# Experts in plain fp32 on column groups, each matrix loaded by halves of its rows, results added by five indirect transfers

## The chip, the cores and the metric

The kernel runs on one core of a Trainium2 chip. The metric is device time in microseconds for one execution of the whole program. Before the change the median of three runs is 3200.23 us (3194.36 to 3200.39). Numbers of views and waits come from one profiled execution.

## What is computed

One inference step of a two-layer backbone for 512 sample tokens and 128 prompt tokens of width 1024. Each layer has a mixer (four branches, gates, an output product) and then a feed-forward part of 16 experts, which is what the change is about:

```
aff = softmax(tok @ router_w)                       # per token over 16 experts
top_aff, top_idx = top_k(aff.T, cap)                # each expert takes 64 sample and 16 prompt tokens
xe  = tok[top_idx]
hid = silu(xe @ w_gate[e]) * (xe @ w_up[e])         # 1024 -> 1024
ye  = (hid @ w_down[e]) * top_aff
out = zeros.at[top_idx].add(ye)                     # a token can be taken by several experts
```

Everything is fp32. An expert has three matrices of 1024 x 1024, 4 MB each; the 16 experts of a layer are 201 MB of weights, read once per layer.

## The kernel before

The program is a loop over two layers, each a row of stages with a barrier between them: norm, projections, latent heads, attention, ssm, merge, norm, `router` (line 1709), `choose` (1838), `experts` (1878), `add_experts` (2142). Every engine has its own instruction list, and semaphores order them.

`router` writes the token rows to `tok_rows` in DRAM, clears `sum_rows` in DRAM and starts the first expert loads. `choose` finds for every expert the 80 token numbers (`rows`, 64 of samples and then 16 of prompts) and their weights. `experts` does the products. `add_experts` reads `sum_rows` back and adds it to x.

In `experts` the 80 tokens of an expert are the stationary operand and the weights stream past as the moving one, 512 columns at a time. A plain fp32 matmul is avoided: a weight is split into a high part in fp32r (ScalarE's copy, line 2045) and the rest (VectorE's subtraction, line 2095), the tokens and the hidden rows likewise (2049 and 2100, 2061 and 2119), and three fp32r matmuls (1999 to 2001) replace one.

The unit of work is half the columns of one matrix: 2 MB, loaded by one transfer of SP (`load_expert`, line 247, pieces of 2 KB) into one of four slots of `expert_raw`. `unit` (1993) does it in two halves of k, 24 matmuls in all. Six units are an expert. The order on TensorE for expert e is: up(e), gate(e+1) with the transposes of e's hidden rows between its two units, down(e), and the transposes of the tokens of e+2. SP loads into a slot once VectorE has finished the low parts of the unit in it (`lo_ready`).

Between the products: ScalarE takes tanh of the gate sums (2053), VectorE multiplies by the gate (2106) and by the up sums (2113), TensorE transposes the hidden rows (2008), ScalarE scales the result by the token's weight into `ye` (2072). POOL gathers token rows by an indirect transfer (1967), two experts ahead, and adds `ye` to `sum_rows` by another one that accumulates in DRAM (1978), 80 rows of 4 KB; before the next gather it waits for that add to land.

Names in the traces: `h` is the memory in which the gathered tokens, `ye` and the hidden rows lie; `ps` is PSUM; `w_hi`, `w_lo`, `xe_hi`, `hid_hi` and so on are the split parts. `Modulation.products` (338) and the attention's `values` (967) already use groups of 32 and of 64 columns of TensorE.

## Time and profile before

| | |
|---|---|
| median of 3 runs | 3200.23 us |
| profiled execution | 3198.26 us |
| its span, first to last instruction | 3196.4 us |
| TensorE busy | 2791.0 us (87%), 17628 matmul records |
| VectorE busy | 2016.8 us (63%) |
| ScalarE busy | 1449.4 us (45%) |
| POOL busy | 416.3 us (13%) |
| DMA | 644.97 MB, mean 202 GB/s |
| mean granted TensorE clock | 0.93 of 2.4 GHz |

The span is nearly the whole time, so a stage's length can be read from the trace directly. Busy TensorE is not TensorE at its peak, since matmuls overlap one another; the spacing of starts is what tells how fast it goes. A fp32 matmul appears as two records, a fp32r matmul and a transpose as one. The tables give instructions their line in the kernel; windows are in us from the span's start.

### The profile page before, as it was taken

The page shows a single profiled execution, that of the slowest core. Times are in us where ns is not written, and L with a number is a line of the kernel's source. Part 1 is how long each engine was busy: PE and PEld are TensorE (multiplying, and loading weights), DVE is VectorE, ACT ScalarE, POOL GpSimd, SP SyncE. Part 2 cuts the span into 40 slices and gives each one's busy share as a digit, 9 for nine tenths or more (in the row PEclk, how much of TensorE's full clock was granted, in tenths as well). Part 3 has the DMA queues.
Part 4 walks back from the last instruction along what each step waited for, and adds up shares of the span by engine and source line. Part 5 has one row for each costly group of instructions (what it writes and reads, how often), then busy time and mean ns, then how long its engine had stood idle before and what let it go on. Part 6 is the DMA issues. An engine that isn't in the chain of part 4 may idle for free. (4 is left out here: it accounts for less than half of the span.)

```text
span 3196.4 us, 44902 instructions
## 1 busy us (share of the span) xinstructions
PE 2791.0 (87%) x17628; PEld 2189.9 (69%) x17628; DVE 2016.8 (63%) x2629; ACT 1449.4 (45%) x1672; POOL 416.3 (13%) x150
## 2 busy tenths in 40 slices
PE   4997999797886999999669889996978589999994
PEld 3995878696764666666459767886878466666662
DVE  2225656756626998998542265566665478988983
ACT  3112544432223777777331134443321257777771
POOL 1001000010010233433010100000100103334310
PEclk7998999898987999999889989998989789999997
DMA  6211212135736999999432112222283779999992
GB/s 234 80 41 63 65 54 65 45 87 199 302 136 260 367 389 387 390 386 386 158 115 74 54 47 56 61 59 62 75 336 145 279 255 384 386 393 384 384 354 74
DMA packets 378679, 644.97 MB, mean 202 GB/s; under 512 B 13072, under 2 KB 124816, under 8 KB 377616
## 3 DMA queue, kind: packets, MB, share of 16 engines
q1 hardware_dynamic: 372368, 621.71, 53.6%
q0 software_dynamic: 6144, 20.98, 2.8%
q8 instruction: 112, 1.84, 0.2%
q14 instruction: 55, 0.45, 0.0%
HBM read 591.13 MB, written 51.51 MB: 201 GB/s over the span
## 5 line engine op out<-in xcount | busy, mean ns | idle before, releaser
L2095 DVE TENSOR_TENSOR w_lo<-expert_raw,w_hi 128x2048 fp32r<-128x2048 f32 x384 | 868.0, 2287 | 90.5 <-ACT w_hi L2045 90.2
L2045 ACT ACTIVATE w_hi<-expert_raw 128x2048 fp32r<-128x2048 f32 x384 | 736.7, 1920 | 337.3 <-PE ps L2001 278.4
L1999 PE MATMUL ps<-w_hi,xe_hi 128*80 128x512 f32 x1024 | 408.2, 399 | 11.2 <-DVE xe_lo L2100 11.2
L2000 PE MATMUL ps<-w_lo,xe_hi 128*80 128x512 f32 x1024 | 404.8, 395 | 0.0
L2001 PE MATMUL ps<-w_hi,xe_lo 128*80 128x512 f32 x1024 | 400.6, 391 | 0.0
L1967 POOL DMA_INDIRECT h<-tok_rows,rows x32 | 263.8, 8242 | 289.7 <-DMA sum_rows<-h,rows 183.1
L539 PE MATMUL ps<-h_hi,in_w_hi 128*128 128x320 f32 x640 | 199.6, 312 | 41.3 <-DVE h_lo L591 41.3
L1999 PEld LDWEIGHTS ps<-w_hi,xe_hi 128*80 128x80 f32 x1024 | 152.4, 149 | 92.4 <-DVE xe_lo L2100 11.7
L818 PE MATMUL ps<-h_hi,attention_gate_w_hi 128*128 128x320 f32 x640 | 206.7, 323 | 9.1 <-DVE attention_gate_w_lo L805 9.1
L2001 PEld LDWEIGHTS ps<-w_hi,xe_lo 128*80 128x80 f32 x1024 | 152.6, 149 | 86.3 <-issue 1.8
L1584 PE MATMUL ps<-branch_mix_hi,merge_w_hi 128*128 128x320 f32 x512 | 165.9, 324 | 51.9 <-DVE merge_w_lo L1663 45.3
L1999 PE MATMUL ps<-w_hi,hid_hi 128*80 128x512 f32 x512 | 204.1, 399 | 3.3 <-DVE hid_lo L2119 3.3
L2000 PEld LDWEIGHTS ps<-w_lo,xe_hi 128*80 128x80 f32 x1024 | 152.7, 149 | 76.9 <-issue 1.4
L2000 PE MATMUL ps<-w_lo,hid_hi 128*80 128x512 f32 x512 | 203.4, 397 | 0.0
L2001 PE MATMUL ps<-w_hi,hid_lo 128*80 128x512 f32 x512 | 201.3, 393 | 0.0
L540 PE MATMUL ps<-h_lo,in_w_hi 128*128 128x320 f32 x640 | 199.3, 311 | 0.0
L541 PE MATMUL ps<-h_hi,in_w_lo 128*128 128x320 f32 x640 | 198.9, 311 | 0.0
L819 PE MATMUL ps<-h_lo,attention_gate_w_hi 128*128 128x320 f32 x640 | 198.9, 311 | 0.0
L820 PE MATMUL ps<-h_hi,attention_gate_w_lo 128*128 128x320 f32 x640 | 198.8, 311 | 0.0
L585 DVE TENSOR_TENSOR in_w_lo<-in_raw,in_w_hi 128x2048 fp32r<-128x2048 f32 (+1 forms) x24 | 55.1, 2297 | 183.7 <-ACT in_w_hi L603 183.7
L1066 DVE TENSOR_REDUCE row_max<-ps 128x1 f32<-128x640 f32 (+1 forms) x128 | 88.5, 692 | 116.7 <-PE ps L944 116.7
L1585 PE MATMUL ps<-branch_mix_lo,merge_w_hi 128*128 128x320 f32 x512 | 161.9, 316 | 0.0
(305 smaller groups left out, 5447.7 us busy)
## 6 DMA issues: line engine op xcount, KB each, us to landing
expert_raw<-in_exp_w_gate SPq DMA_DIRECT2D x64, 2048.0 KB, 10.8
expert_raw<-in_exp_w_up SPq DMA_DIRECT2D x64, 2048.0 KB, 10.2
expert_raw<-in_exp_w_down SPq DMA_DIRECT2D x64, 2048.0 KB, 11.2
merge_mod_raw<-in_mod_w SPq DMA_DIRECT2D x16, 2048.0 KB, 11.7
in_raw<-in_w_mix SPq DMA_DIRECT2D x20, 1024.0 KB, 5.3
attention_gate_raw<-in_w_in SPq DMA_DIRECT2D x80, 256.0 KB, 3.4
gate_tanh_back<-gate_rows SPq DMA_DIRECT2D x64, 320.0 KB, 8.0
n_mod_raw<-in_mod_w SPq DMA_DIRECT2D x8, 2048.0 KB, 15.4
```

The source lines that it names most:

```text
L539: pe.matmul(dst, whi[:, s, k, cols], h_hi[:, k, a:z], start=(k == 0), stop=False)
L540: pe.matmul(dst, whi[:, s, k, cols], h_lo[:, k, a:z], start=False, stop=False)
L541: last = pe.matmul(dst, wlo[:, s, k, cols], h_hi[:, k, a:z], start=False, stop=(k == KD - 1))
L818: pe.matmul(self.out, self.whi[:, m % 3, k, :], self.h_hi[:, kk, toks], start=(kk == 0), stop=False)
L819: pe.matmul(self.out, self.whi[:, m % 3, k, :], self.h_lo[:, kk, toks], start=False, stop=False)
L820: last = pe.matmul(self.out, self.wlo[:, m % 3, k, :], self.h_hi[:, kk, toks], start=False, stop=(kk == KD - 1))
L1967: pool.indirect_dma_start(out=xe[:, e % 2, :], out_offset=None, in_=io["tok_rows"], in_offset=bass.IndirectOffsetOnAxis(rows[:, e:e + 1], ...
L1999: pe.matmul(ps[0:SLOTS, bank, :], hi[:, k, :], whi[:, s, w, :], start=(k == 0), stop=False)
L2000: pe.matmul(ps[0:SLOTS, bank, :], hi[:, k, :], wlo[:, s, w, :], start=False, stop=False)
L2001: last = pe.matmul(ps[0:SLOTS, bank, :], lo[:, k, :], whi[:, s, w, :], start=False, stop=(k == KD - 1))
L2045: act.activation(whi[:, (2 * i + kh) % SPLIT], raw[:, i % RAW, KH * kh:KH * kh + KH], ACT.Copy).then_inc(hi_ready, 1)
L2095: v.tensor_tensor(wlo[:, s], raw[:, i % RAW, KH * kh:KH * kh + KH], whi[:, s].bitcast(F32), ALU.subtract).then_inc(lo_ready, 1)
```

## The change

The split is gone. Tokens and hidden rows are used in fp32, and so are the weights, straight from `expert_raw`. To make up for the slower fp32 pass, the two kinds of tokens go separately. The 64 sample tokens are stationary in a group of 64 columns of TensorE, and the two halves of a matrix's columns (512 each) go to the two groups: `samples`. The 16 prompt tokens, padded with zeros to 32, use groups of 32 columns, and the four quarters (256 each) go to the four groups: `prompts`. The sums of an expert then lie in PSUM as 128 partitions by 768: 512 with samples (the partition tells token and half) and 256 with prompts (token and quarter). The gate arithmetic works on that shape, the hidden rows are transposed in six blocks of 128 and not in eight of 80, and the result is added from that shape: one indirect transfer for the samples, which sees `sum_rows` as rows of 512, and four for the prompts, which see it as rows of 256.

A load now fetches half the rows of a matrix (four slices of k, all 1024 columns, pieces of 4 KB), into one of six slots of `expert_raw`, which go by pairs: gate of expert 0 and afterwards every down in the first, up in the second, the other gates in the third. Four of them and not two are started at the router's end. SP loads a slot once TensorE has used it (`used`). At the start of the stage SP copies `rows` and `weight` to the partitions where the groups need them (nine small transfers), VectorE clears the padding and works out the numbers of half and quarter rows, and ScalarE waits for the copies before its first work.

```diff
-IN_RAW, EXPERT_RAW = [P, 2, KD, 2 * P + 4], [P, 4, KD, 512]
+IN_RAW, EXPERT_RAW = [P, 2, KD, 2 * P + 4], [P, 6, KD // 2, D]
...
+SLOT_COLS = CAP_S + 32
+EXPERT_LOADS = (NE + 1, NE, NE - 1)
 def load_expert(sp, io, g, layer, e, matrix, half, slot):
     src = io[("exp_w_gate", "exp_w_up", "exp_w_down")[matrix]][bass.ds(layer, 1)]
     src = src[:, e:e + 1] if isinstance(e, int) else src[:, bass.ds(e, 1)]
-    columns = slice(half * 512, (half + 1) * 512)
-    sp.dma_start(g["expert_raw"][:, slot], src.rearrange("l e (k p) n -> p (l e k) n", p=P)[:, :, columns]).then_inc(
+    k = half * (KD // 2)
+    sp.dma_start(g["expert_raw"][:, slot], src.rearrange("l e (k p) n -> p (l e k) n", p=P)[:, k:k + KD // 2, :]).then_inc(
...
-            for u in range(2):
-                load_expert(sp, io, g, layer, 0, u // 2, u % 2, u)
+            first = [(e, matrix, u) for e, matrix in ((0, 0), (0, 1), (1, 0)) for u in range(2)]
+            for slot in range(2):
+                load_expert(sp, io, g, layer, *first[slot], slot)
...
+        xt = sb("xe_t", [P, 2, KD, WIDE])
+        ht = sb("hid_t", [P, HID // P, P])
+        hid = sb("hid", [P, 2, HID])
+        yq = sb("y_quarters", [P, 2, HID])
+        rows_s, rows_p = sb("rows_sample", [P, NE], mybir.dt.uint32), sb("rows_prompt", [CAP_P, 5, NE], mybir.dt.uint32)
+        weight_s, weight_p = (sb(n, [P, NE]) for n in ("weight_sample", "weight_prompt"))
...
         def _(sp):
-            def load(e, matrix, half, slot):
-                load_expert(sp, io, g, layer, e, matrix, half, slot)
+            sp.wait_ge(blank, 1)
+            for half in range(2):
+                lo = 64 * half
+                copies.start(sp, rows_s[lo:lo + CAP_S], rows[0:CAP_S])
+                copies.start(sp, weight_s[lo:lo + CAP_S], weight[0:CAP_S])
+            copies.start(sp, rows_p[:, 4], rows[CAP_S:SLOTS])
+            for r in range(4):
+                copies.start(sp, weight_p[32 * r:32 * r + CAP_P], weight[CAP_S:SLOTS])
+            def load(e, matrix, pair, done):
+                for u in range(2):
+                    sp.wait_ge(used, done + u)
+                    load_expert(sp, io, g, layer, e, matrix, u, 2 * pair + u)
             def expert(e, q, j, before_last, last_one):
-                if last_one:
-                    return
-                for u in range(UNITS):
-                    sp.wait_ge(lo_ready, halves(e, u + 1))
-                    slot = part(j, u) % RAW
-                    if u < NEXT0:
-                        load(e, DOWN, u, slot)
-                    elif u < DOWN0:
-                        load(e + 1, UP, u - NEXT0, slot)
-                    elif before_last:
-                        load(e + 1, DOWN, u - DOWN0, slot)
-                    else:
-                        load(e + 2, GATE, u - DOWN0, slot)
-            for u in range(LEAD):
-                sp.wait_ge(lo_ready, 2 * (u + 1))
-                load(1, GATE, u, u)
+                load(e, DOWN, 0, e * 6 + 1)
+                if not last_one:
+                    load(e + 1, UP, 1, e * 6 + 3)
+                    if not before_last:
+                        load(e + 2, GATE, 2, e * 6 + 5)
...
+            pool.wait_ge(pieces_ready, 6)
             for e in range(NE):
                 if e + 2 < NE:
                     pool.wait_ge(xe_turned, e + 1)
                     gather(e + 2)
-                pool.wait_ge(ye_ready, e + 2)
-                pool.indirect_dma_start(out=io["sum_rows"], out_offset=bass.IndirectOffsetOnAxis(rows[:, e:e + 1], 0),
-                                        in_=ye[:, e % 2, :], in_offset=None, compute_op=ALU.add).then_inc(rows_added, 16)
-                pool.wait_ge(rows_added, layer * (16 * NE) + 16 * (e + 1))
+                pool.wait_ge(y_copied, e + 2)
+                pool.indirect_dma_start(out=io["sum_rows"].rearrange("t (a n) -> (t a) n", a=2),
+                                        out_offset=bass.IndirectOffsetOnAxis(rows_s[:, e:e + 1], 0),
+                                        in_=yq[:, e % 2, 0:512], in_offset=None, compute_op=ALU.add).then_inc(rows_added, 16)
+                for r in range(4):
+                    pool.indirect_dma_start(out=io["sum_rows"].rearrange("t (a n) -> (t a) n", a=4),
+                                            out_offset=bass.IndirectOffsetOnAxis(rows_p[:, r, e:e + 1], 0),
+                                            in_=yq[32 * r:32 * r + CAP_P, e % 2, 512:HID], in_offset=None, compute_op=ALU.add).then_inc(rows_added, 16)
+                pool.wait_ge(rows_added, layer * (80 * NE) + 80 * (e + 1))
...
-            def unit(e, j, u, bank, hi, lo):
-                for kh in range(2):
-                    s = (2 * part(j, u) + kh) % SPLIT
-                    pe.wait_ge(lo_ready, halves(e, u) + (kh + 1))
-                    for k in range(KH * kh, KH * kh + KH):
-                        w = k % KH
-                        pe.matmul(ps[0:SLOTS, bank, :], hi[:, k, :], whi[:, s, w, :], start=(k == 0), stop=False)
-                        pe.matmul(ps[0:SLOTS, bank, :], hi[:, k, :], wlo[:, s, w, :], start=False, stop=False)
-                        last = pe.matmul(ps[0:SLOTS, bank, :], lo[:, k, :], whi[:, s, w, :], start=False, stop=(k == KD - 1))
-                    last.then_inc(split_free, 1)
-            def turn_hidden(e):
+            def samples(pair, u, bank, left):
+                for k in range(u * KH, (u + 1) * KH):
+                    for half in range(2):
+                        pe.matmul(ps[64 * half:64 * half + 64, bank, :], left(k), raw[:, 2 * pair + u, k % KH, 512 * half:512 * half + 512],
+                                  start=(k == 0), stop=(k == KD - 1))
+            def prompts(pair, u, bank, left):
+                for k in range(u * KH, (u + 1) * KH):
+                    for q in range(4):
+                        last = pe.matmul(ps[32 * q:32 * q + 32, bank, 0:256], left(k), raw[:, 2 * pair + u, k % KH, 256 * q:256 * q + 256],
+                                         start=(k == 0), stop=(k == KD - 1))
+                last.then_inc(used, 1)
...
+            def products(pair, bank, left, nth, between=None):
+                for u in range(2):
+                    loaded(pair, u, nth)
+                    samples(pair, u, bank, left[0])
+                    if u == 1 and between:
+                        between()
+                    prompts(pair, u, bank + 1, left[1])
...
+            def turn_hidden(e, j):
                 pe.wait_ge(hid_ready, e + 1)
-                pe.wait_ge(ye_ready, e + 1)
-                for k in range(KD):
-                    last = pe.transpose(ps[:, 6 + k // 4, (k % 4) * SLOTS:(k % 4 + 1) * SLOTS], hid[:, k * P:(k + 1) * P],
-                                        cst[0:SLOTS, C_ID:C_ID + SLOTS])
+                pe.wait_ge(y_copied, e + 1)
+                for b in range(HID // P):
+                    last = pe.transpose(both(D_BANK)[:, b * P:(b + 1) * P], hid[:, j, b * P:(b + 1) * P], cst[:, C_ID:C_ID + P])
                 last.then_inc(hid_turned, 1)
...
-                for i in range(2):
-                    unit(e, j, UP0 + i, 2 + i, xhi[:, j], xlo[:, j])
+                products(1, U_BANK, tokens(j), q * 32 + 16 * (j + 1))
                 if last_one:
-                    turn_hidden(e)
+                    turn_hidden(e, j)
                 else:
-                    pe.wait_ge(xlo_ready, e + 2)
+                    pe.wait_ge(xt_ready, e + 2)
                     pe.wait_ge(gated, e + 1)
-                    unit(e, j, NEXT0, 0, xhi[:, 1 - j], xlo[:, 1 - j])
-                    turn_hidden(e)
-                    unit(e, j, NEXT0 + 1, 1, xhi[:, 1 - j], xlo[:, 1 - j])
-                pe.wait_ge(hlo_ready, e + 1)
-                for i in range(2):
-                    unit(e, j, (NEXT0 if last_one else DOWN0) + i, 6 + i, hhi, hlo)
+                    products(2, G_BANK, tokens(1 - j), q * 32 + 16 * (j + 1), lambda: turn_hidden(e, j))
+                pe.wait_ge(ht_ready, e + 1)
+                products(0, D_BANK, (lambda k: ht[:, k % 4, 64 * (k // 4):64 * (k // 4) + 64],
+                                     lambda k: ht[:, 4 + k % 2, 32 * (k // 2):32 * (k // 2) + 32]), q * 32 + 16 * (j + 2))
...
+                act.activation(ht[:].rearrange("p a b -> p (a b)"), both(D_BANK), ACT.Copy).then_inc(ht_ready, 1)
...
+                nth = bass.ds(e, 1) if not isinstance(e, int) else slice(e, e + 1)
+                act.activation(yq[:, j, 0:512], ps[:, D_BANK, :], ACT.Copy, scale=weight_s[:, nth])
+                act.activation(yq[:, j, 512:HID], ps[:, D_BANK + 1, 0:HID - 512], ACT.Copy, scale=weight_p[:, nth]).then_inc(y_copied, 1)
...
+            act.wait_ge(blank, 2)
+            act.wait_ge(copies.sem, 16 * 9)
...
+            v.memset(weight_p[:], 0.0).then_inc(blank, 1)
+            v.memset(xt[:, :, :, SLOTS:WIDE], 0.0).then_inc(blank, 1)
+            v.wait_ge(copies.sem, 16 * 9)
+            for half in range(2):
+                part = rows_s[64 * half:64 * half + CAP_S]
+                v.tensor_scalar(part, part, 2.0, float(half), ALU.mult, ALU.add).then_inc(pieces_ready, 1)
+            for r in range(4):
+                v.tensor_scalar(rows_p[:, r], rows_p[:, 4], 4.0, float(r), ALU.mult, ALU.add).then_inc(pieces_ready, 1)
```

How the lists of instructions change, at the two places that matter most. TensorE, inside an expert, around the transposes of the hidden rows (`ps` is PSUM, `cst` the identity, `h` the hidden rows). Before:

```order
L1999 MATMUL ps<-w_hi,xe_hi 80x512
L2000 MATMUL ps<-w_lo,xe_hi 80x512
L2001 MATMUL ps<-w_hi,xe_lo 80x512
L2008 MATMUL ps<-cst,h 128x80 x8
L1996 REGISTER_ALU
L1999 MATMUL ps<-w_hi,xe_hi 80x512
L2000 MATMUL ps<-w_lo,xe_hi 80x512
L2001 MATMUL ps<-w_hi,xe_lo 80x512
```

After (`xe_t` and `hid_t` are the transposed tokens and hidden rows, and x8, x16 are runs of equal rows):

```order
L1994 MATMUL ps<-expert_raw,xe_t 64x512 x8
L2000 MATMUL ps<-expert_raw,xe_t 32x256 x16
L1994 MATMUL ps<-expert_raw,xe_t 64x512 x8
L2024 MATMUL ps<-cst,hid 128x128 x6
L2000 MATMUL ps<-expert_raw,xe_t 32x256 x16
L2006 ISA
L1994 MATMUL ps<-expert_raw,hid_t 64x512 x8
L2000 MATMUL ps<-expert_raw,hid_t 32x256 x16
L1994 MATMUL ps<-expert_raw,hid_t 64x512 x8
L2000 MATMUL ps<-expert_raw,hid_t 32x256 x16
```

Runs of three 80 x 512 matmuls are replaced by runs of eight 64 x 512 and sixteen 32 x 256 ones, in turn, and the transposes now stand between samples and prompts of the gate's second half.

POOL, the first experts of the stage (`h` takes the gathered tokens). Before:

```order
L1967 DMA h<-tok_rows,rows 80x1024 x3
L1978 DMA sum_rows<-h,rows 640x1024
L1980 ISA
L1967 DMA h<-tok_rows,rows 80x1024
L1978 DMA sum_rows<-h,rows 640x1024
L1980 REGISTER_ALU
```

After (`y_quarters` is the scaled result in its 128 by 768 shape):

```order
L1958 DMA h<-tok_rows,rows 80x1024 x3
L1970 DMA sum_rows<-y_quarters,rows_sample 1280x512
L1974 DMA sum_rows<-y_quarters,rows_prompt 2560x256 x4
L1977 ISA
L1958 DMA h<-tok_rows,rows 80x1024
L1970 DMA sum_rows<-y_quarters,rows_sample 1280x512
L1974 DMA sum_rows<-y_quarters,rows_prompt 2560x256 x4
L1977 REGISTER_ALU
```

Each expert's one add to `sum_rows` has become one and four more.

## Rows read from the trace of the kernel before

**Rows 1.** Stages: busy us (count) of PE, PEld, DVE, ACT, POOL; clock, DMA share, GB/s

```profile
1100.00:1508.00 408.00, 408.00 (x1911) 267.18 (x1910) 366.51 (x191) 308.94 (x191) 146.68 (x24) 1.00 1.05 388
```

**Rows 2.** Who waited for whom, 1050 to 1500 us (total, times, longest)

```profile
ACT w_hi L2045 <- PE ps L2001: 108.2, 131, 0.8
```

**Rows 3.** Timeline, two experts (start us, us, engine, line, operation)

```profile
1199.78 0.39 PE L2001 MATMUL ps<-w_hi,xe_lo 128*80 128x512 f32 x1
...
1214.94 0.39 PE L2001 MATMUL ps<-w_hi,xe_lo 128*80 128x512 f32 x1
...
1201.46 2.35 POOL L1978 DMA_INDIRECT sum_rows<-h,rows  x1 [14.92 <-ACT h L2072]
...
1235.66 2.35 POOL L1978 DMA_INDIRECT sum_rows<-h,rows  x1 [15.01 <-ACT h L2072]
```

**Rows 4.** Timeline, PE, transposes of the hidden rows

```profile
1215.17 0.72 PE L2008 MATMUL ps<-cst,h 80*128 80x80 f32 x8
1215.68 0.43 PE L1999 MATMUL ps<-w_hi,xe_hi 128*80 128x512 f32 x1
```

**Rows 5.** Timeline, start of the expert stage in layer 0

```profile
1006.36 1.33 PE L1989 MATMUL ps<-cst,h 80*128 80x80 f32 x8 [6.01 <-DMA h<-tok_rows,rows]
...
1008.80 0.68 ACT L2049 ACTIVATE xe_hi<-ps 128x640 fp32r<-128x640 f32 x1
...
1013.28 0.71 PE L1999 MATMUL ps<-w_hi,xe_hi 128*80 128x512 f32 x1 [5.59 <-DVE xe_lo L2100]
```

**Rows 6.** DMA issues: KB each, median us from issue to landing

```profile
router_w<-in_router_w SPq DMA_DIRECT2D x2, 64.0 KB, 2.4
```

**Rows 7.** Timeline, end of the expert stage in layer 0

```profile
1550.94 0.39 PE L2001 MATMUL ps<-w_hi,xe_lo 128*80 128x512 f32 x1
...
1555.52 1.21 DVE L2113 SCALAR_TENSOR_TENSOR h<-h,ps 80x1024 f32<-80x1024 f32 x1
1556.78 1.33 PE L2008 MATMUL ps<-cst,h 80*128 80x80 f32 x8 [5.46 <-DVE h L2113]
...
1559.77 0.72 PE L1999 MATMUL ps<-w_hi,hid_hi 128*80 128x512 f32 x1 [1.65 <-DVE hid_lo L2119]
...
1574.94 1.40 POOL L1978 DMA_INDIRECT sum_rows<-h,rows  x1 [18.04 <-ACT h L2072]
1584.09 4.45 SPq L2154 DMA_DIRECT2D sum_tok<-sum_rows  x5
```

**Rows 8.** Timeline, PE, plain fp32 at full width, latent heads

```profile
295.91 5.34 PE L721 MATMUL ps<-wukv,kt 128*128 128x256 f32 x24
```

**Rows 9.** Timeline, PE, narrow products between wide ones in the merge

```profile
780.10 0.31 PE L1586 MATMUL ps<-branch_mix_hi,merge_w_lo 128*128 128x320 f32 x1
780.34 1.96 PE L338 MATMUL ps<-merge_mod_raw,silu 128*32 128x128 f32 x64
782.22 0.41 PE L1584 MATMUL ps<-branch_mix_hi,merge_w_hi 128*128 128x320 f32 x1
```

**Rows 10.** Timeline, PE, pairs of 64 columns in the attention

```profile
322.66 0.38 PE L954 MATMUL ps<-cst,x 128*128 128x128 f32 x2
322.98 1.31 PE L967 MATMUL ps<-x,v 128*64 128x128 f32 x20
324.22 0.33 PE L954 MATMUL ps<-cst,x 128*128 128x128 f32 x1
```

**Rows 11.** Timeline, PE, row groups of 64 and 32 in the attention

```profile
405.86 0.49 PE L944 MATMUL ps<-kn,qn 64*128 64x128 f32 x4
406.28 0.49 PE L944 MATMUL ps<-kt,qr 32*128 32x128 f32 x4
```

**Rows 12.** Busy time in windows of 5 us (as rows 1)

```profile
965.00:970.00 5.00, 4.10 (x37) 3.44 (x36) 3.09 (x9) 3.23 (x5) 0.00 (x0) 1.00 1.02 419
...
1205.00:1210.00 5.00, 5.00 (x23) 3.22 (x22) 3.35 (x3) 3.32 (x3) 0.00 (x0) 1.00 1.05 342
1210.00:1215.00 5.00, 5.00 (x24) 3.19 (x23) 5.00 (x3) 3.69 (x2) 4.29 (x1) 1.00 1.05 409
```

More of the change, by code:

```diff
@@ L1747, in _ @@
                 sp.dma_start(io["tok_rows"][t * P:(t + 1) * P, :], htok[:, t, :]).then_inc(rows_out, 16)
-            for u in range(2, EXPERT_RAW[1]):
-                load_expert(sp, io, g, layer, 0, u // 2, u % 2, u)
+            for slot in range(2, EXPERT_RAW[1]):
+                load_expert(sp, io, g, layer, *first[slot], slot)
             sp.wait_ge(rows_out, 16 * 2 * NT)
@@ new lines, in loaded, with tokens @@
+            def loaded(pair, u, nth):
+                pe.wait_ge(raw_loaded[2 * pair + u], layer * (16 * EXPERT_LOADS[pair]) + nth)
+            def products(pair, bank, left, nth, between=None):
[5 more added lines that the diff above has]
+                    prompts(pair, u, bank + 1, left[1])
+            def tokens(j):
+                return (lambda k: xt[:, j, k, 0:CAP_S]), (lambda k: xt[:, j, k, CAP_S:WIDE])
@@ L2032, in _ @@
-            for i in range(LEAD):
-                unit(0, 0, i - LEAD, i, xhi[:, 0], xlo[:, 0])
+            pe.wait_ge(xt_ready, 1)
+            products(0, G_BANK, tokens(0), 16)
             turn_tokens(0, 1)
@@ L2038, in _, with tokens @@
         def _(act):
-            def split_hi(e, q, j, u):
-                i = part(j, u)
-                act.wait_ge(raw_loaded[i % RAW], layer * (16 * NE * UNITS // RAW) + (q * (16 * 2 * UNITS // RAW) + 16 * (i // RAW + 1)))
-                for kh in range(2):
-                    act.wait_ge(split_free, halves(e, u) + (kh + 1))
-                    act.activation(whi[:, (2 * i + kh) % SPLIT], raw[:, i % RAW, KH * kh:KH * kh + KH], ACT.Copy).then_inc(hi_ready, 1)
-            def tokens_hi(nth, j):
+            def tokens(nth, j):
@@ L2055, in expert, with gate @@
+            def gate(done, j):
+                act.wait_ge(used, done)
+                act.activation(hid[:, j, :], both(G_BANK), ACT.Tanh, scale=0.5).then_inc(gate_tanh, 1)
             def expert(e, q, j, before_last, last_one):
+                act.wait_ge(hid_turned, e + 1)
+                act.activation(ht[:].rearrange("p a b -> p (a b)"), both(D_BANK), ACT.Copy).then_inc(ht_ready, 1)
                 if not last_one:
[L2057 to L2058 removed]
@@ L2070, in expert @@
-                act.wait_ge(split_free, halves(e, DOWN0 if last_one else UNITS) + SPLIT)
+                    gate(e * 6 + 6, 1 - j)
+                act.wait_ge(used, e * 6 + (6 if last_one else 8))
                 act.wait_ge(ye_free, e + 1)
-                act.activation(ye[:, j, :], pair(6, SLOTS, D), ACT.Copy, scale=weight[:, bass.ds(e, 1)] if not isinstance(e, int)
-                               else weight[:, e:e + 1]).then_inc(ye_ready, 1)
+                nth = bass.ds(e, 1) if not isinstance(e, int) else slice(e, e + 1)
@@ L2103, in gate @@
-            def gate(nth):
+            def gate(nth, j):
                 v.wait_ge(gate_tanh, nth)
-                v.scalar_tensor_tensor(out=hid, in0=hid, scalar=1.0, in1=pair(0, SLOTS, FF), op0=ALU.add, op1=ALU.mult).then_inc(gated, 1)
+                v.scalar_tensor_tensor(out=hid[:, j, :], in0=hid[:, j, :], scalar=1.0, in1=both(G_BANK), op0=ALU.add, op1=ALU.mult).then_inc(gated, 1)
             def expert(e, q, j, before_last, last_one):
-                if not last_one:
-                    split_lo(e, j, NEXT0)
-                v.wait_ge(split_free, halves(e, NEXT0) + SPLIT)
+                v.wait_ge(used, e * 6 + 4)
```

110 lines of the change are left out of this document (22 added, 88 removed).

## Prediction

> **What bounds the kernel now.** I began with the table of stages. The expert stage (lines 1878 to 2139), which is all that the change touches besides its first loads, runs from about 1000 to 1584 us in layer 0, and again at the end of layer 1. In its steady part TensorE is busy for all of 408 us at the full granted clock of 1.00 (2.4 GHz), while the DMA engines show a share of 1.05 and 388 GB/s [rows 1]. Both look full, so the waits decide. ScalarE, which opens every weight, waits 131 times for TensorE to free a split buffer [rows 2], and no engine waits for a weight load in that stretch. TensorE is the engine that sets the pace.
>
> One expert takes 1235.66 - 1201.46 = 34.2 us, and from the first to the last matmul shown there are 66 steps in 15.16 us, 0.2297 us each [rows 3]. An expert has 3 products x 48 matmuls: 144 x 0.2297 = 33.1 us; its two times eight transposes take 0.51 us each time (and 0.05 us on the matmul behind them) [rows 4]: 34.2 in all, nothing missing. From the first matmul to the end of the last "up" product it is 1550.94 + 0.23 - 1013.28 = 537.9 us [rows 5, 7]. I call this stretch the body.
>
> **The body after the change.** Every product loses its 48 fp32r matmuls of 512 columns. In their place are, for each of 8 slices of k, two fp32 matmuls of 512 columns in column groups of 64 (the samples) and four of 256 columns in groups of 32 (the prompts). All of the splitting on ScalarE and VectorE goes too, but that was hidden work and is costed at nothing.
>
> Do such groups run beside one another? An fp32 matmul leaves two records, and at full width 24 of 256 columns take 5.34 us [rows 8]: 0.22 us each, 2 cycles of 2.4 GHz a column and a little. A record of 128 columns is 106.7 ns. Sixty-four such records in groups of 32 take 782.22 - 780.34 = 1.88 us, the way in excluded [rows 9]; one behind the other they would need 6.8 us, four at a time 1.71. Twenty records in groups of 64 take 1.24 us against 2.13 in a row and 1.07 in pairs [rows 10]. So both kinds overlap fully. The 1.88 us in groups of 32, less 0.09 for the way out, are 16 steps of 0.112 us, some 6 ns over 106.7; I carry 6 ns a step.
>
> One product is then 16 steps x (426.7 + 6) ns for the samples and 16 x (213.3 + 6) ns for the prompts: 6.92 + 3.51 = 10.43 us, against 48 x 0.2297 = 11.03 before. The body holds 47 products (16 gate, 16 up, 15 down): 490.2 us. Token transposes stay, 16 x 0.51 = 8.2 us. Those of the hidden rows become six of 128 columns instead of eight of 80: 0.51 x (6 x 128)/(8 x 80) = 0.61 us, 15 times, 9.2 us.
>
> New is the change between widths of column groups: samples, prompts, samples, prompts makes four changes for a product, and each of 31 groups of transposes adds one: 4 x 47 + 31 = 219. **Their price is the term that I know least.** Going in, the matmul at 780.10 should be done at 780.25 and the narrow one starts at 780.34: 0.09 us [rows 9]. The last transpose before the pairs starts at 322.77, is done at 322.88, and the pair starts at 322.98: 0.10 us; going out, 1.24 - 1.07 - 10 x 0.006 = 0.11 us [rows 10]. On the other side stand short stretches between row groups of 64 and 32: two steps of 0.107 us take 406.28 - 405.86 = 0.42, so 0.2 us a change [rows 11]. There the second step also waits for a 128-column weight load; the new steps of 213 and 427 ns are long enough to hide theirs. I take 0.10 and keep 0.20 as the upper end: 219 x 0.10 = 21.9 us.
>
> Of the old body, 47 products (518.2 us) and 31 times 0.56 us of transposes leave 2.3 us, which I put down to its start at 1.2 GHz (the first matmul is 0.71 us long [rows 5], one at 2.4 GHz 0.39 [rows 3]); the new body starts as cold. Body after: 490.2 + 8.2 + 9.2 + 21.9 + 2.3 = 531.8 us, against 537.9: **-6.1 us a layer**.
>
> **Will the weights come in time?** An expert moves 12.58 MB of weights and 0.66 MB of gathered and scattered rows. The new body gives it (531.8 - 2.3)/15.7 = 33.8 us, so 392 GB/s. The rows show 409 GB/s with the present 2 KB pieces when only weights move, 342 in a window with a scatter, and 419 in a window of 4 KB rows [rows 12]. Pieces become 4 KB, and six halves of a matrix are held instead of four. With all six loaded at the start the PE is five loads, some 28 us, ahead; even if an expert's transfers took 1 us more than the products, 15 us of that would be used. I charge nothing. The skill has a rule against this: the Trainium skill (DMA: Bandwidth & Descriptors, Specifications) gives a limit of some 358 GB/s for a core from HBM, at which an expert's 13.24 MB would take 37 us and transfers, not products, would bind both kernels. The trace disagrees, with 388 GB/s held over 408 us [rows 1].
>
> **The start of the stage.** Before, the first product waits for ScalarE, busy with splits, and for the low half of the tokens: transposes from 1006.36 to 1007.69, ScalarE's high half of 0.68 us, and only at 1013.28, released by VectorE's xe_lo, the first product [rows 5]. Now one ScalarE copy of 0.68 us is enough, so 1008.5 at best. But ScalarE also waits for nine small copies of rows and weights that SP issues. Five issues take 4.45 us in the row of the summed tokens [rows 7], 0.89 each, and a small load lands in 2.4 us [rows 6]: from 1001 that is 1011.4, and the first product at 1012.5. The five are 512 KB transfers and these are 1 to 4 KB, so I lean to the low end, 1009.6: **-3.7 us a layer** (bounds -0.8 and -4.8). Queued behind that wait on ScalarE stands only the first tokens' copy; POOL's gathers do not wait for it.
>
> **The tail.** From the end of the last "up" to the last scatter's issue it is 1574.94 - 1551.17 = 23.8 us: VectorE is still splitting and starts the gate product at 1555.52, transposes 1556.78, hi and lo, first matmul 1559.77, again at 1.2 GHz (0.72 us long) [rows 7]. From there 15.2 us are 48 x 0.2297 = 11.0, 2.3 for the clock and 1.8 for the end of the pipeline, the scaled copy and the issue. After: gate product 0.1 + 0.91 (1.21 x 768/1024), transposes 0.8, one copy 0.9 (0.68 x 768/640 and a start), the down product 10.4 + 0.4, and 1.8 again: 15.3 us, if idle times of 1 us keep the clock up. **-8.5 us a layer**; -6.2 if the clock falls.
>
> Then five indirect adds stand in the place of one, issued one behind the other on POOL. One of 80 rows took 1.40 us with VectorE quiet [rows 7] and 2.35 with it busy [rows 3]; four more of 16 rows cost between nothing (their landing overlaps) and 5.6 us. I take **+3**. In the steady part five of even 2.35 us are 12 us of POOL's 34, and the next expert's products cover them.
>
> **Sum.** -6.1 - 3.7 - 8.5 + 3 = -15.3 us a layer, -30.6 for both. The profiled execution took 3198.3 us (2 us under the median of the three runs), so 3167.7. With half of that offset the forecast is **3169 us**. About 0.2% (6 us) is what a measurement of this kernel can tell from no change.
>
> **Rivals.**
> The changes of width cost 0.2 us, not 0.1. For it: that is what the shortest stretches show [rows 11], and nothing in the trace goes from 64 to 32 columns and back every two or three microseconds. Against it: [rows 9, 10]. It adds 0.1 x 219 x 2 = 44 us: 3213, slower. It decides from 0.17 us a change, where the gain is gone (30/438 above 0.10). The Trainium skill (TensorEngine Tiling (Array Packing), Key Properties) says that changing the tiling mode, unlike changing the tile, drains TensorE; it names no price, and by that rule each of the 219 is paid in full. The trace agrees that each one costs something. Chance 0.18.
>
> The transfers become the bound. The scatter goes from 80 pieces of 4 KB to 128 of 2 KB and 64 of 1 KB, and the dip around a scatter is already deep [rows 12]. A window with one lacks (409 - 342) GB/s x 5 us = 0.34 MB, 0.8 us, and its own 0.33 MB take as much: 1.6 us. If that goes by pieces (x 2.4, +2.2 us) and 4 KB weight pieces are no faster, an expert's transfers need some 36.4 us; over 15 experts they fall 39 us behind, the head start covers 28, and 11 us a layer stay: 3169 + 22 = 3191, about no change on either side of 0.2%. Against it: 419 GB/s in the 4 KB window. Chance 0.14.
>
> Groups of 64 with 512 columns do not overlap (the trace has them with 128 only). Samples would cost double, 3 x 6.9 us an expert: +650 us, 3820. Chance 0.02, against [rows 10].
>
> **Numbers.** The forecast's case has 0.66. Its own range is 3152 (steps without the 6 ns, the scatters hidden) to 3192 (0.14 us a change, a cold tail). Taking in the rivals except the last, the range is 3152 to 3213. Faster by over 0.2%: 0.66; within: 0.14; slower: 0.20.
>
> **What would show it.** Right: a period of about 33.8 us between the scatters of two experts, TensorE with idle time only where the width changes, first product near 1009.6 in stage time, some 15 us from the last up to the scatter. A period of 36 with gaps between narrow and wide matmuls is the first rival; TensorE waiting for expert_raw is the second. I am wrong outright if the products alone show more than 10.8 us each.

## The result, and the profile after

The changed kernel took **3188.1 us** (median; 3186.1 to 3190.5), the kernel before 3199.2 us beside it: a ratio of 0.9968, 95% interval 0.9958 to 0.9978. It is faster by 11 us, or 0.3%, where 30 us were forecast. The gain is small, but the interval lies wholly below 1. The profiled execution took 3189.6 us (before: 3198.3), its span is 3187.5.

First the page of the changed kernel, as far as it answers to the table of before:

```profile
PE 2786.0 (87%) x22172; PEld 1893.9 (59%) x22172; DVE 1096.5 (34%) x2197; ACT 723.6 (23%) x1320; POOL 325.2 (10%) x278
...
L1974 POOL DMA_INDIRECT sum_rows<-y_quarters,rows_prompt x128 | 165.7, 1295 | 39.0 <-issue 39.0
```

VectorE and ScalarE have lost the splits. POOL has gained 128 small adds of 1.3 us. Its total fell all the same, from 416 to 325 us, because a gather's record (line 1967 before, 1958 now) is 0.95 us long on average where it was 8.24. No run isolates why, and POOL was not the bound.

The table of stages, for the stretch of [rows 1] (columns as there):

```profile
1100.00:1508.00 408.00, 408.00 (x3616) 158.06 (x3612) 22.90 (x24) 39.19 (x60) 90.44 (x71) 1.00 1.03 387
```

and POOL's timeline, two samples' adds one expert apart (start, duration, instruction; before: [rows 3]):

```profile
1195.76 1.56 POOL L1970 DMA_INDIRECT sum_rows<-y_quarters,rows_sample  x1 [20.28 <-ACT y_quarters L2067]
...
1229.96 1.56 POOL L1970 DMA_INDIRECT sum_rows<-y_quarters,rows_sample  x1 [19.99 <-ACT y_quarters L2067]
```

An expert takes 1229.96 - 1195.76 = 34.20 us, exactly what it took before. TensorE is still busy all the time at 1.00, and the DMA share is as full as it was. So the steady part gained nothing. TensorE's timeline shows an expert from its second "up" half on (a fp32 matmul counts twice here: samples x16 are 8 matmuls and prompts x32 are 16, four slices of k each; x6 are the hidden rows' transposes, x8 the tokens'):

```profile
1200.35 3.65 PE L1994 MATMUL ps<-expert_raw,xe_t 128*64 128x512 f32 x16
1203.94 1.93 PE L2000 MATMUL ps<-expert_raw,xe_t 128*32 128x256 f32 x32
1205.80 3.65 PE L1994 MATMUL ps<-expert_raw,xe_t 128*64 128x512 f32 x16
1209.39 1.93 PE L2000 MATMUL ps<-expert_raw,xe_t 128*32 128x256 f32 x32
1211.25 3.65 PE L1994 MATMUL ps<-expert_raw,xe_t 128*64 128x512 f32 x16
1214.84 0.88 PE L2024 MATMUL ps<-cst,hid 128*128 128x128 f32 x6
1215.64 1.93 PE L2000 MATMUL ps<-expert_raw,xe_t 128*32 128x256 f32 x32
...
1228.40 0.77 PE L1986 MATMUL ps<-cst,h 80*128 80x80 f32 x8
1229.11 3.22 PE L1994 MATMUL ps<-expert_raw,xe_t 128*64 128x512 f32 x14
```

From start to start, four slices of samples take 1203.94 - 1200.35 = 3.59 us and four of prompts 1.86: a product is 10.90 us, against 11.03 before. The hidden rows' transposes take 0.80, the tokens' 0.71: 3 x 10.90 + 1.51 = 34.2.

The start of the stage in layer 0 (before: [rows 5]); TensorE's timeline, then ScalarE's:

```profile
1005.89 1.33 PE L1986 MATMUL ps<-cst,h 80*128 80x80 f32 x8 [6.02 <-DMA h<-tok_rows,rows]
1009.39 6.57 PE L1994 MATMUL ps<-expert_raw,xe_t 128*64 128x512 f32 x16 [2.17 <-ACT xe_t L2052]
1015.89 1.93 PE L2000 MATMUL ps<-expert_raw,xe_t 128*32 128x256 f32 x32
```

```profile
1008.56 0.70 ACT L2052 ACTIVATE xe_t<-ps 128x640 f32<-128x640 f32 x1 [36.87 <-DMA weight_prompt<-weight]
```

The nine small copies do hold ScalarE, by about a microsecond. The first product starts 3.50 us behind the first transposes, against 6.92 before. Its samples take 6.50 us instead of 3.59, at a granted clock of 0.50 (1.2 GHz) up to 1013 us, behind a stretch in which TensorE was mostly idle.

The end of the stage in layer 0: TensorE, POOL, and the queue's first load of the next stage (before: [rows 7]):

```profile
1545.23 1.93 PE L2000 MATMUL ps<-expert_raw,xe_t 128*32 128x256 f32 x32
1548.24 0.87 PE L2024 MATMUL ps<-cst,hid 128*128 128x128 f32 x6 [1.08 <-DVE hid L2088]
1550.09 3.65 PE L1994 MATMUL ps<-expert_raw,hid_t 128*64 128x512 f32 x16 [0.97 <-ACT hid_t L2060]
```

```profile
1562.45 1.55 POOL L1970 DMA_INDIRECT sum_rows<-y_quarters,rows_sample  x1 [16.83 <-ACT y_quarters L2067]
1564.31 1.30 POOL L1974 DMA_INDIRECT sum_rows<-y_quarters,rows_prompt  x1 [0.30 <-issue]
...
1569.11 1.29 POOL L1974 DMA_INDIRECT sum_rows<-y_quarters,rows_prompt  x1 [0.30 <-issue]
```

```profile
1580.63 2.52 SPq L2117 DMA_DIRECT2D sum_tok<-sum_rows  x5
```

From the last "up" (its end, 1547.09) to the first add it is 15.4 us, with the clock kept at 1.00, against 23.8 before. But from that add to the next stage's load it is 18.2 us, against 1584.09 - 1574.94 = 9.15 before. The sum for layer 0, each from its own rows:

| us, layer 0 | forecast | measured |
|---|---|---|
| start (start of TensorE's wait for the gather to first product: 12.9, now 9.5) | -3.7 | -3.4 |
| body (first product to end of last "up": 537.9, now 537.7) | -6.1 | **-0.2** |
| tail (end of last "up" to first add: 23.8, now 15.4) | -8.5 | -8.4 |
| adds (first add to next load: 9.15, now 18.2) | +3 | **+9.0** |
| sum | -15.3 | -3.0 |

In layer 1 the same four are -3.7, -1.7, -8.4 and +9.3 (its adds take 18.2 us, 8.9 before); the body does better there by 1.5 us because the first samples take 4.99 us and not 6.50. Two terms of the four are off: the body by 5.9 and 4.4 us, the adds by 6.0 and 6.3, 22.6 us for both layers. Missing are 19.5 us by the medians and 21.9 by the profiled executions (8.7 gained of 30.6), so nothing of size lies elsewhere.

### The profile page after: what moved, and what is told of

The parts are those of the page before. It is cut to its first block and busy times, and to the rows that moved or that the text cites. A ratio compares the mean times of both kernels' runs of the same rounds, so it can differ in the third digit from the quotient of the medians.

```text
span 3187.5 us, 52462 instructions
## 1 busy us (share of the span) xinstructions
PE 2786.0 (87%) x22172; PEld 1893.9 (59%) x22172; DVE 1096.5 (34%) x2197; ACT 723.6 (23%) x1320; POOL 325.2 (10%) x278
## 5 line engine op out<-in xcount | busy, mean ns | idle before, releaser
L1994 PE MATMUL ps<-expert_raw,xe_t 128*64 128x512 f32 x2048 | 472.0, 603 | 4.0 <-ACT xe_t L2052 4.0
L1994 PEld LDWEIGHTS ps<-expert_raw,xe_t 128*64 128x64 f32 x2048 | 136.7, 137 | 268.9 <-issue 266.3
L2000 PE MATMUL ps<-expert_raw,xe_t 128*32 128x256 f32 x4096 | 247.6, 382 | 0.0
L1994 PE MATMUL ps<-expert_raw,hid_t 128*64 128x512 f32 x1024 | 233.8, 598 | 1.9 <-ACT hid_t L2060 1.9
L2000 PEld LDWEIGHTS ps<-expert_raw,xe_t 128*32 128x32 f32 x4096 | 120.0, 109 | 150.7 <-issue 84.8
L1974 POOL DMA_INDIRECT sum_rows<-y_quarters,rows_prompt x128 | 165.7, 1295 | 39.0 <-issue 39.0
L1587 PE MATMUL ps<-branch_mix_hi,merge_w_lo 128*128 128x320 f32 x512 | 161.7, 316 | 0.0
L819 PE MATMUL ps<-h_hi,ssm_gate_w_hi 128*128 128x320 f32 x384 | 129.2, 336 | 30.9 <-ACT ssm_gate_tanh L831 17.0
L540 PEld LDWEIGHTS ps<-h_hi,in_w_hi 128*128 128x128 f32 x640 | 121.6, 190 | 41.6 <-DVE in_w_lo L586 41.6
L1585 PEld LDWEIGHTS ps<-branch_mix_hi,merge_w_hi 128*128 128x128 f32 x512 | 99.5, 194 | 60.7 <-DVE merge_w_lo L1664 53.0
```

Source lines behind the costliest of these rows:

```text
L540: pe.matmul(dst, whi[:, s, k, cols], h_hi[:, k, a:z], start=(k == 0), stop=False)
L819: pe.matmul(self.out, self.whi[:, m % 3, k, :], self.h_hi[:, kk, toks], start=(kk == 0), stop=False)
L1585: pe.matmul(dst, whi_, hi, start=first, stop=False)
L1587: return pe.matmul(dst, wlo_, hi, start=False, stop=last)
L1974: pool.indirect_dma_start(out=io["sum_rows"].rearrange("t (a n) -> (t a) n", a=4), out_offset=bass.IndirectOffsetOnAxis(rows_p[:, r, e:e + ...
L1994: pe.matmul(ps[64 * half:64 * half + 64, bank, :], left(k), raw[:, 2 * pair + u, k % KH, 512 * half:512 * half + 512], start=(k == 0), sto ...
```

## Experiments

Two questions. Is the period of 34.2 us TensorE's, with a change of width at 0.15 us instead of 0.10, or is it that of the transfers, which look just as full? And what makes the five adds cost 9 us?

The differences to the changed kernel (3188.1 us) are between medians of different sittings. The kernel before, run beside each, had medians from 3197.0 to 3199.2 us, so a difference of 2 us says nothing. The ratios are to the kernel before.

**Fewer changes of width.**

```
-  u = 0, 1: samples(u), prompts(u)
+  samples(0), prompts(0), prompts(1), samples(1)
```

> Same work as the changed kernel, but each product runs samples, prompts, prompts, samples, so that it changes the width of its column groups twice and not four times. Theory A (TensorE sets the pace and a change costs about 0.15 us): 2 x 0.15 us less for each of 96 products, -29 us against the changed kernel's 3188.1, so 3159, and a period of 33.3 us instead of 34.2. Theory B (the transfers set the pace at some 387 GB/s and the width changes are hidden): no change of the period beyond 0.1 us, 3185 to 3189.

Measured: 3165.4 us (3163.5 to 3168.0), ratio 0.9901 (0.9886 to 0.9916), 22.7 us faster than the changed kernel. POOL's adds are 33.49 us apart. TensorE's timeline:

```profile
1202.85 3.66 PE L2002 MATMUL ps<-expert_raw,xe_t 128*32 128x256 f32 x64
1206.44 0.88 PE L2029 MATMUL ps<-cst,hid 128*128 128x128 f32 x6
...
1217.86 3.65 PE L1994 MATMUL ps<-expert_raw,hid_t 128*64 128x512 f32 x16
1221.44 0.78 PE L1986 MATMUL ps<-cst,h 80*128 80x80 f32 x8
1222.14 3.65 PE L1994 MATMUL ps<-expert_raw,xe_t 128*64 128x512 f32 x16
1225.73 3.66 PE L2002 MATMUL ps<-expert_raw,xe_t 128*32 128x256 f32 x64
```

Sixty-four records of prompts in one go take 3.59 us where two times 32 took 2 x 1.86. The gain is short of the 29 us expected for two reasons. I miscounted: the tokens' transposes now stand between samples and samples, where there would be no change without them. And at the tail of both layers the first samples of the last "down" take 5.35 us here and 3.65 in the changed kernel, since the clock fell there (see "The copies out of the way"). An expert goes from 14 changes (12, and one more for each group of transposes) to 9 (6 + 1 + 2), and its period from 34.20 to 33.49 us, so 0.71 / 5 = 0.14 us each.

**More changes of width.**

```
-  samples(k = 0..3), prompts(k = 0..3)
+  samples(k = 0, 1), prompts(k = 0, 1), samples(k = 2, 3), prompts(k = 2, 3)
```

> Same work as the changed kernel, but samples and prompts take turns every two slices: eight changes of width for a product, not four. Theory A: +4 x 0.15 us for each of 96 products, +58 us, 3246, period 36.0 us. Theory B: the transfers have little slack for it either way, since TensorE is close behind; a part of the 58 us is hidden, less than 3240.

Measured: 3246.6 us (3243.4 to 3250.9), ratio 1.0154 (1.0140 to 1.0168): 58.4 us slower than the changed kernel, all of theory A's 58. The period is 36.0 us. Its timeline on TensorE:

```profile
1208.64 1.94 PE L1994 MATMUL ps<-expert_raw,xe_t 128*64 128x512 f32 x8
1210.51 1.07 PE L2000 MATMUL ps<-expert_raw,xe_t 128*32 128x256 f32 x16
1211.51 1.94 PE L1994 MATMUL ps<-expert_raw,xe_t 128*64 128x512 f32 x8
```

This splits a stretch into steps and a change. Samples: 4 steps take 1.87 us, 8 take 3.59, so a step is 1.72 / 4 = 0.430 and what is left 0.15. Prompts: 4 steps 1.00 us, 8 steps 1.86, 16 steps 3.59: a step is 0.216 us and what is left 0.14. So a change costs **0.14 to 0.15 us** in either direction, and a step some 3 ns over its columns (426.7 and 213.3 ns), not 6. What TensorE does in a change no run shows.

**Lighter traffic.**

```
-  load_expert: 4 slices of k
+  in the loop: 3 slices of k
```

> Leaves out the last quarter of every weight load inside the stage's loop (the products read what stands there), TensorE's work unchanged. Theory A: the period stays within 0.2 us of 34.2 and the time within 6 us of 3188, since TensorE never waited for weights. Theory B: the period falls to what the products need, and the time by 10 us or more. It also shows a step of the products with lighter traffic: if 0.429 us falls towards 0.427, traffic does not matter to a step.

Measured: 3188.5 us (3182.8 to 3191.8), 0.9972 (0.9963 to 0.9982), the same as with all of the weights. The stage table:

```profile
1100.00:1508.00 408.00, 408.00 (x3616) 158.16 (x3614) 22.87 (x24) 39.24 (x60) 90.19 (x72) 1.00 0.85 296
```

A quarter less to move, 296 GB/s instead of 387, and the period is still 34.2 us with half products of 3.59 and 1.86. The transfers did not set the time, and lighter traffic did not shorten a step.

**Less for TensorE.**

```
-  prompts: 4 slices of each half matrix
+  2 slices
```

> Leaves out half of the prompts' matmuls (two of each four slices), loads unchanged. TensorE needs 3 x 16 x 0.113/2... that is 3 x 32 records' worth of 1.75 us less, some 5.2 us an expert. Theory A: the period falls only to where the transfers bind: with 12.58 MB of weights and 0.66 MB of rows it shows that floor, 32 us or less if over 409 GB/s can be held (about -60 us in all). Theory B: the transfers bind already and the period stays at 34 us, the time within 10 us of 3188.

Measured: 3112.4 us (3107.3 to 3120.0), 0.9729 (0.9714 to 0.9743), 76 us faster than the changed kernel. Two of its adds, and its waits in the stretch from 1100 to 1508 us (engine and tile, what it waited for, us in total, times, longest):

```profile
1207.59 1.56 POOL L1970 DMA_INDIRECT sum_rows<-y_quarters,rows_sample  x1 [19.08 <-ACT y_quarters L2067]
1240.66 1.56 POOL L1970 DMA_INDIRECT sum_rows<-y_quarters,rows_sample  x1 [19.27 <-ACT y_quarters L2067]
```

```profile
PEld ps L1994 <- DMA expert_raw<-in_exp_w_gate: 34.8, 20, 2.7
...
PEld ps L1994 <- DMA expert_raw<-in_exp_w_down: 21.1, 21, 1.8
```

Here TensorE does wait for weights, some 20 times for the gate halves and as often for the down halves. Between the first four samples' adds of the stage the periods are 29.1 us, while the loads that stand ahead are used up; the later ones lie between 32.4 and 34.1 us, and the eight from 1174.63 us on are 33.2 on average. That is the transfers' own period: 13.24 MB in that are 399 GB/s. The fast start and the shorter tail are why the whole gains more than 31 times the difference in period. My expectation's floor of 32 us or less was too low. In the changed kernel no engine waits for a weight in the stage's steady part, and TensorE is 1.0 us slower than that floor. The two theories are settled by this: TensorE sets the pace, with little room below it.

**Without the prompts' adds.**

```
-  four indirect adds of 16 rows
```

> Leaves out the four prompt adds of every expert (the prompts' rows get nothing), so one indirect add of 128 rows of 2 KB stands where one of 80 rows of 4 KB stood in the kernel before. Theory A (the small adds are paid one behind the other on POOL, 1.3 us and a gap each, and their landing behind that): from the last scatter's issue to the next stage's first load it falls from 18.2 us to some 9 to 10, in both layers, 3188 - 17 = 3171; the period stays 34.2 us. Theory B (the longer tail comes from the samples' add in 128 smaller pieces, or from later traffic): it stays above 14 us, time 3180 or more.

Measured: 3165.5 us (3165.2 to 3175.4), 0.9909 (0.9895 to 0.9923), 22.6 us faster than the changed kernel. POOL and the queue at the end of layer 0:

```profile
1563.25 1.54 POOL L1970 DMA_INDIRECT sum_rows<-y_quarters,rows_sample  x1 [23.23 <-ACT y_quarters L2063]
```

```profile
1571.52 2.46 SPq L2113 DMA_DIRECT2D sum_tok<-sum_rows  x5
```

8.3 us from the add to the load (8.4 in layer 1), less than the 9.15 of the kernel before with its 80 rows of 4 KB. The samples' smaller pieces cost nothing. All of the growth belongs to the four small adds: 9.9 us in layer 0 (9.8 in layer 1), 2.5 each. That makes 19.7 us of the 22.6; the profiled execution (3169.6 us) lies 20.0 below that of the changed kernel, and the five runs spread over 10 us.

**The prompts' adds in one.**

```
-  for r in range(4): indirect add of 16 rows, index rows_p[:, r], from yq[32 * r:32 * r + 16]
+  indirect add of 128 rows, index rows_q (4 x row + r; 64 rows of padding go behind the sum), from yq[:, 512:768]
```

> The four prompt adds of an expert become one of 128 quarter rows, whose 64 rows of padding go to rows behind the sum (one more zeroing transfer, one small copy fewer). Theory A by number of adds: three issues of 1.3 us and gaps of 0.3 less, 4.8 us a layer, and where the landing also grows with each transfer up to 7: 3173 to 3179. Theory B (what counts is the bytes and pieces, of which there are more now): no gain or a loss, 3186 or more.

Measured: 3170.8 us (3169.8 to 3172.2), 0.9920 (0.9906 to 0.9933), 17.4 us faster than the changed kernel.

```profile
1559.94 1.54 POOL L1970 DMA_INDIRECT sum_rows<-y_quarters,rows_sample  x1 [21.40 <-ACT y_quarters L2066]
1561.79 1.54 POOL L1973 DMA_INDIRECT sum_rows<-y_quarters,rows_quarter  x1 [0.30 <-issue]
```

```profile
1570.77 2.47 SPq L2118 DMA_DIRECT2D sum_tok<-sum_rows  x5
```

10.8 us in both layers, against 18.2: 2 x 7.35 = 14.7 us. Some 1.5 of the rest is the clock: here the first samples take 5.05 us at the start of the stage in layer 0, there 6.57.

**The samples' add in two.**

```
-  indirect add of 128 rows of 512 columns
+  two of 128 rows of 256 columns
```

> The kernel of run merged with the samples' add in two of 256 columns: three adds for an expert in all, the same bytes in 256 pieces of 1 KB instead of 128 of 2 KB. From the last scatter to the next stage's load one add took 8.3 us, two 10.8, five 18.2. Theory A (some 2.5 us for every add, whatever its rows): 13.3 us, 3171 + 5 = 3176. Theory B (the pieces count, each of the four small ones being costly by chance of where they land): with 384 pieces against 192 in the five adds it is above 18 us, or without any effect of the number it stays near 11.

Measured: 3176.6 us (3176.2 to 3178.0), 0.9932 (0.9918 to 0.9946), 5.9 us slower than merged. The last adds:

```profile
1559.72 1.54 POOL L1971 DMA_INDIRECT sum_rows<-y_quarters,rows_sample  x1 [19.56 <-ACT y_quarters L2067]
...
1563.41 1.54 POOL L1974 DMA_INDIRECT sum_rows<-y_quarters,rows_quarter  x1 [0.30 <-issue]
```

```profile
1573.30 2.56 SPq L2121 DMA_DIRECT2D sum_tok<-sum_rows  x5
```

13.6 us. So one add takes 8.3 us, two 10.8, three 13.6, five 18.2: 2.5 us for each of four small ones, 2.5 and 2.8 for one more of 128 rows.

Where this time goes can be read on POOL. Each record and its gap are 1.6 us (16 rows) or 1.85 us (128 rows). The stage's end (line 106, the close of the block) then has an instruction DRAIN on POOL, which is not counted as busy. For one add, two, three and five, in layer 0 (count, shortest, median and longest in ns, first and last start; the longest is the one that starts first):

```profile
L106 POOLq DRAIN  x2: 34/1350/2666, 1568.1 to 1571.5; - x2
...
L106 POOLq DRAIN  x2: 34/2003/3972, 1566.1 to 1570.7; - x2
...
L106 POOLq DRAIN  x2: 34/2656/5279, 1567.3 to 1573.3; - x2
...
L106 POOLq DRAIN  x2: 34/3963/7892, 1572.0 to 1580.6; - x2
```

It takes 2.67, 3.97, 5.28 and 7.89 us: 1.31 us more for each further add, of 16 rows or 128, and the same within 0.01 us in layer 1. The next load starts some 0.7 us behind its end. What overlaps is the landing: from the last add's record to this DRAIN it is 3.3 us with one add and 1.6 with five. From one add to five that is +6.4 (records and gaps) - 1.7 + 5.2 (DRAIN) = 9.9 us, all of the growth.

**The copies out of the way.**

```
-  ScalarE: wait for the nine copies, tokens, gate, tokens
+  ScalarE: tokens, gate, tokens, wait for the nine copies
```

> ScalarE waits for the nine small copies behind its first three instructions instead of ahead of them. Theory A (the copies hold the first product by about a microsecond): tokens' copy right behind the transposes, first product 0.9 us earlier in each layer, 3186. Theory B (something else, such as the first weights or the gather, is just as late): 3188.

Measured: 3188.8 us (3185.4 to 3190.3), 0.9973 (0.9962 to 0.9985): no difference. The mechanism is there: the first product stands 2.26 us behind the first transposes instead of 3.50. From the start of TensorE's wait for the gather to the next stage's load, layer 0 takes 579.7 us against 580.8, 1.1 less, although its first samples, too, take 5.21 us and not 6.50. Layer 1 takes 1.1 us more. Both layers lose 1.6 us at their tail, on TensorE:

```profile
1547.42 5.23 PE L1994 MATMUL ps<-expert_raw,hid_t 128*64 128x512 f32 x16 [0.97 <-ACT hid_t L2060]
...
3110.66 5.25 PE L1994 MATMUL ps<-expert_raw,hid_t 128*64 128x512 f32 x16 [0.98 <-ACT hid_t L2060]
```

There the changed kernel has 3.65 us, both times. The granted clock is 0.90 and 0.67 in the two windows of 4 us from 1544 on and 0.81 and 0.76 in those from 3108 on, where the changed kernel's is 1.00 in all four. Behind the same idle stretches (1.1 and 1.0 us) the clock fell in one kernel and held in the other. The profiles of the changed kernel and of the ten kernels made from it have 22 such tails, and it fell in 7: in both layers of runs early and two_changes, and in layer 0 alone of runs three, eight_changes and half_prompts. So it goes both ways within one execution; what decides it stays open, and 1 us a layer is too little to see beside it.

**Three together**: the order of run two_changes, the add of run merged, and the early start.

> The order samples, prompts, prompts, samples, the merged prompt add and the early start together. If the savings add up: -22.7 (measured for the order alone), -10 to -14 for the adds, -2 for the start: 3150 to 3154. If the transfers become the bound once TensorE needs 33.5 us an expert, it stays nearer 3160.

Measured: 3149.6 us (3145.5 to 3152.3), 0.9855 (0.9840 to 0.9870), period 33.49. The savings add up: 38.5 us together, against 22.7 + 17.4 - 0.7 = 39.4 for the single runs.

**One change of width for a product.**

```
+  samples(0), samples(1), prompts(0), prompts(1), and the next product prompts first
```

> The kernel of run three with one change of width for a product: samples, samples, prompts, prompts, and the next product the other way round, so that a product begins at the width with which the last one ended. Changes in an expert fall from 9 (6, and 3 around transposes) to 3 + 2 x 1 + 1 for transposes, some 6: at 0.15 us each the products need 33.0 us an expert instead of 33.5. Theory A (TensorE alone sets the pace): period 33.0 to 33.1 us, 3150 - 13 = 3137. Theory B (the transfers' own period, 33.0 us in the run with half of the prompts' matmuls, binds here, and the first half of a matrix is given back half a product later): the period stays near 33.4, TensorE shows waits for expert_raw, 3143 to 3150.

Measured: **3136.1 us** (3133.1 to 3138.0), 0.9803 (0.9790 to 0.9817): theory A's 3137. Its stage table and POOL's timeline:

```profile
1100.00:1508.00 408.00, 408.00 (x3756) 173.40 (x3756) 23.59 (x25) 40.91 (x62) 48.27 (x36) 1.00 1.03 395
```

```profile
1187.83 1.55 POOL L1970 DMA_INDIRECT sum_rows<-y_quarters,rows_sample  x1 [21.18 <-ACT y_quarters L2069]
1220.90 1.56 POOL L1970 DMA_INDIRECT sum_rows<-y_quarters,rows_sample  x1 [21.01 <-ACT y_quarters L2069]
```

33.07 us an expert, TensorE busy throughout, and over the whole body of layer 0 only two waits for a weight, 0.5 us together. This is at the transfers' floor of run half_prompts. A further saving on TensorE would meet them; that was not tried.

The same trace shows that it is the width that costs, not the next product with its other bank and weights. Here the prompts of "up" and of the next gate follow one another:

```profile
1194.01 7.11 PE L2000 MATMUL ps<-expert_raw,xe_t 128*32 128x256 f32 x128
1201.06 0.88 PE L2026 MATMUL ps<-cst,hid 128*128 128x128 f32 x6
```

They take 7.05 us from start to start: 32 steps of 0.216 us and one change of 0.14.

## Why the prediction was off

The direction was right, and the range held the time. Of the 30 us forecast 11 came.

- **What bounds the kernel.** Right: TensorE. After the change both look full at 34.2 us, but a quarter less traffic changed nothing (run less_weight) and each change of width added shows in full (run eight_changes). For the kernel before it rests on the waits alone; no run lightened that one. The Trainium skill (DMA: Bandwidth & Descriptors, Specifications) lists some 358 GB/s from HBM for a core, which I read as a limit here. The same page says, under its table of measured bandwidth, that this is the share of each core when both cores of an HBM domain stream. Here one core ran, and it held 395 GB/s over 408 us in run one_change.
- **The step that failed in the body** is the term "219 x 0.10 = 21.9 us". A change costs 0.14 to 0.15 us, so it is 32 us. My "6 ns a step" was too much on the other side: a product without its changes is 10.90 - 4 x 0.145 = 10.32 us, not 10.43, some 5 us a layer less. The cold start took 2.9 us in layer 0, not 2.3 (1.4 in layer 1). Together 10 - 5 + 0.6, nearly all of the 5.9 us in layer 0. The 0.10 was the mean of two excursions in and out of groups; the short stretches that stood against it [rows 11] gave 0.2. The truth lay between the ends, and at my own limit for the favourable case, below the 0.17 us at which the gain would have been gone. By my sign "wrong outright if the products alone show more than 10.8 us" the case is between: 10.90 us with their four changes, 10.32 without. The Trainium skill's sentence (TensorEngine Tiling (Array Packing), Key Properties) that a change of mode drains TensorE fits, with 0.14 to 0.15 us as its price here.
- **Groups overlap.** Right: samples in two groups take 0.43 us a step, not twice that.
- **Transfers hold.** Right: no weight was late. The dip around a scatter is there (run half_prompts: 358 GB/s from 1210 to 1215 us, 420 to 424 in the three windows of 5 us before), but the transfers' own period is 33.2 us, not the 36.4 of the second rival.
- **The start.** Right: -3.4 for -3.7. The nine copies cost a microsecond, as leaned.
- **The tail.** Right: 15.4 us for 15.3, and the clock stayed up. That last was partly luck: behind the same idle stretches it fell in 7 of 22 tails, at 1.6 to 1.7 us each.
- **The second step that failed** is "I take +3" for the five adds. They cost +9.0. I had bounded four more by "nothing" and 5.6 us, the POOL records alone (4 x 1.40). The price lies above that bound: 2.5 us each to the next stage's load. The landing does overlap, as I took it. I left out the gap of 0.3 us between issues, and POOL's DRAIN at the end of the stage, which is 7.89 us with five adds and 2.80 (layer 0) and 2.66 us (layer 1) with the one of the kernel before.
- **The range.** It held the time, but its low end was summed wrongly. Steps without the 6 ns are 18 us less and hidden scatters 6, so by those two it should have been 3145 and not 3152. The time lies near the other end, which was made of 0.14 us a change and a cold tail: the changes did cost that, but the tail stayed warm, and the adds, which the range had at +3, cost 12 us more for both layers. That it fell inside is in part terms that cancel.

During the DRAIN nothing moves and no engine works. The changed kernel's table of stages, in a window of 2 us:

```profile
1572.00:1574.00 2.00, 0.00 (x0) 0.00 (x0) 0.00 (x0) 0.00 (x0) 0.00 (x0) 0.50 0.00 0
```

It is the same up to 1580. The wait grows with the number of adds, not with their bytes. Why POOL needs 1.31 us for each of them, behind its wait for all to land, no run shows.

## What to carry to other kernels

When column groups of two widths share a loop, put all work of one width together and let the next block begin at the width where the last one ended: here 14 changes an expert at 0.15 us ate what the cheaper matmuls had saved, and ordering alone gave 23 us, and with one change a product about 36. Price an indirect transfer at the end of a stage by its count, not its bytes (16 or 128 rows of 1 or 2 KB made no difference here), and up to the next stage's first instruction, with the DRAIN at the stage's end, not by its record: merging four adds of 16 rows into one of 128 padded rows gave 17 us. Where TensorE and the DMA engines both look full, lighten each in turn: the one whose relief changes nothing is not the bound, and lightening the other shows how far below the second limit lies.

## What the runs showed that I had not expected

- Each indirect add behind the first delays the end of the stage by 2.5 to 2.8 us, 16 rows or 128. Its record and gap are 1.6 to 1.85 us of POOL, and it lengthens POOL's DRAIN at the end of the stage by 1.31 us (2.67 us with one add, 7.89 with five), while landings overlap.
- A change between groups of 64 and 32 columns takes 0.14 to 0.15 us either way; between two products of the same width, with other banks and weights, there is none (run one_change: 32 steps across two products take 7.05 us, 32 x 0.216 and one change).
- At the tail of the stage the clock fell in 7 of 22 cases and held in 15, behind the same idle stretches of about 1 us; a fall costs 1.6 to 1.7 us.
- One core held 395 GB/s for 408 us with TensorE hardly held up by it (run one_change, 0.5 us in layer 0), and 399 where it was (run half_prompts).
